# TensorE matmuls that nobody reads, issued ahead of its long waits, in a two-layer hybrid decoder trunk

## The reference

```python
for l in range(DEPTH):                       # DEPTH = 2
    h = rms_norm(x, norm_mix[l])
    p = h @ w_in[l]                          # RWKV-7 | gated DeltaNet | sparse MLA | 3 gates
    y_a = rwkv7_branch(...)
    y_b = gated_deltanet_branch(...)
    y_c = dsa_mla_branch(...)
    x = x + (g_a * y_a + g_b * y_b + g_c * y_c) @ w_mix_out[l]
    x = x + memory_xattn(rms_norm(x, norm_xattn[l]), mem_n, ...)
    h = rms_norm(x, norm_ffn[l])
    if l % 2 == 0:
        x = x + swiglu(h, w_gate, w_up, w_down)          # 2816 wide
    else:
        x = x + moe_swiglu(h, router, ...)               # top 2 of 8 experts, each 3584 wide
return rms_norm(x, final_norm)
```

## Time and profile before

| what | value |
|---|---|
| median of 3 runs | 2955.32 us (2954.4 to 2958.49) |
| profiled execution, first to last instruction (span) | 2958.0 us |
| mean granted TensorE clock over the span | 0.954 of 2.4 GHz |
| PE busy | 2588.5 us (88%) |
| VectorE (DVE) busy | 1706.3 us (58%) |
| ScalarE (ACT) busy | 1469.3 us (50%) |
| GpSimd (POOL) busy | 358.2 us (12%) |
| DMA | 531.34 MB, mean 180 GB/s |

### The profile page before, as it was taken

The page is one execution under the profiler, slowest core; times in us unless marked ns, Lnnn a source line. Parts: engine busy times, 40 slices in busy tenths (PEclk is TensorE's granted clock), DMA queues, the critical chain, the costliest instruction groups (busy, mean ns, idle before and its releaser), DMA issues.

```text
span 2958.0 us, 67158 instructions
## 1 busy us (share of the span) xinstructions
PE 2588.5 (88%) x29799; PEld 2117.4 (72%) x29818; DVE 1706.3 (58%) x1983; ACT 1469.3 (50%) x1911; POOL 358.2 (12%) x180
## 2 busy tenths in 40 slices
PE   7988988899797989897988999787898898998986
PEld 6766666777465768665666777557888888888875
DVE  2445463234215542545462233128999999999996
ACT  2233343233224331433343233137888889888885
POOL 0000001000000000000001000001323243324231
PEclk9999999999998999998989999898999999999999
DMA  6411120123216634301121133237999999999994
GB/s 201 135 41 47 31 86 29 37 93 114 95 62 228 202 119 139 100 30 31 58 63 32 58 107 100 100 125 289 388 386 386 386 386 388 382 386 390 385 387 183
DMA packets 304032, 531.34 MB, mean 180 GB/s; under 512 B 18528, under 2 KB 145760, under 8 KB 303360
## 3 DMA queue, kind: packets, MB, share of 16 engines
q1 hardware_dynamic: 303600, 525.99, 50.3%
q10 hardware_dynamic: 144, 1.05, 0.1%
HBM read 524.91 MB, written 2.10 MB: 178 GB/s over the span
## 4 chain that ended last, share of the span: by engine, by line
PE 53%; DVE 33%; ACT 7%; issue 6%; DMA 0%; ACTq 0%; DVEq 0%; SPq 0%
DVE arena L2713 24%; PE bank L799 11%; PE bank L700 9%; PE bank L770 4%; PE bank L1277 4%; PE bank L1236 4%; PE bank L765 3%; PE bank L718 2%; DVE yacc L2721 2%; PE bank L1293 2%; PE bank L644 2%; PE bank L1025 1%; ACT arena L1897 1%; PE bank L875 1%; PE bank L1030 1%
## 5 line engine op out<-in xcount | busy, mean ns | idle before, releaser
L2713 DVE TENSOR_TENSOR arena<-ring,arena 128x2048 bf16<-128x2048 f32 x336 | 833.4, 2525 | 3.8 <-ACT arena L2012 3.8
L2012 ACT ACTIVATE arena<-ring 128x2048 bf16<-128x2048 f32 x336 | 640.4, 1911 | 98.9 <-DMA ring<-in_moe_w_down 30.2
L1378 PE MATMUL bank<-arena 128*128 128x0 bf16 x10752 | 490.6, 209 | 99.4 <-DVE arena L2713 96.3
L1378 PEld LDWEIGHTS bank<-arena 128*128 128x128 bf16 x10752 | 478.6, 100 | 113.7 <-DVE arena L2713 105.3
L799 PE MATMUL bank<-feat,ring 128*128 128x256 f32 x1664 | 433.6, 399 | 8.4 <-ACT ring L1575 2.3
L1527 POOL TENSOR_TENSOR arena<-yacc,arena 128x512 bf16<-128x512 f32 x112 | 300.2, 2692 | 1004.5 <-ACT arena L2035 1004.5
L799 PEld LDWEIGHTS bank<-feat,ring 128*128 128x128 f32 x1664 | 308.6, 196 | 87.3 <-issue 43.1
L1395 PEld LDWEIGHTS bank<-arena 128*128 128x128 bf16 x5376 | 237.8, 98 | 23.0 <-issue 20.0
L1395 PE MATMUL bank<-arena 128*128 128x0 bf16 x5376 | 245.0, 206 | 7.3 <-issue 3.8
L700 PE MATMUL bank<-feat,ring 128*128 128x256 f32 x1056 | 236.8, 388 | 7.7 <-issue 5.7
L700 PEld LDWEIGHTS bank<-feat,ring 128*128 128x128 f32 x1056 | 205.7, 195 | 38.2 <-ACT feat L1566 8.9
(11 more groups left out here) (355 smaller groups left out, 3434.5 us busy)
## 6 DMA issues: line engine op xcount, KB each, us to landing
ring<-in_moe_w_gate SPq DMA_DIRECT2D x112, 1024.0 KB, 8.4
ring<-in_moe_w_up SPq DMA_DIRECT2D x112, 1024.0 KB, 7.9
ring<-in_moe_w_down SPq DMA_DIRECT2D x112, 1024.0 KB, 8.4
ring<-in_w_in SPq DMA_DIRECT2D x76, 1024.0 KB, 5.2
ring<-in_xa_w_kv SPq DMA_DIRECT2D x16, 1024.0 KB, 5.3
ring<-in_ffn_w_gate SPq DMA_DIRECT2D x11, 1024.0 KB, 5.4
ring<-in_ffn_w_up SPq DMA_DIRECT2D x11, 1024.0 KB, 5.4
ring<-in_ffn_w_down SPq DMA_DIRECT2D x11, 1024.0 KB, 7.0
```

The source lines that it names most:

```text
L1378: m = mm(o, w[k // 4][wi][:, k % 4, col:col + P], xg[:, e % 2, xi, k, :].shape_from_register(width[e % 2]), start=i == 0 and k == 0, stop= ...
L2012: sc.activation(w_parts[b][0], ring[:, b * FFN_SLOT:(b + 1) * FFN_SLOT], ACT.Copy).then_inc(S["w_hi"], 1)
L2713: v.tensor_tensor(w_parts[b][1], ring[:, b * FFN_SLOT:(b + 1) * FFN_SLOT], w_parts[b][0], ALU.subtract).then_inc(S["w_lo"], 1)
```

## The change

A helper `unread(n, b)` issues n float32 matmuls of the identity with the 128x512 mask into PSUM bank b. No engine waits for them and none reads what they write. Calls stand at these places of TensorE's program: 8 ahead of the first norm of layer 1; 4 ahead of each norm before the cross attention and before the feed-forward or routing, in both layers; 5 at the opening of DeltaNet, in both layers; 4 ahead of the wait for `ml_n`, in both layers; 8 ahead of the wait for `merged`, in both layers; 11 ahead of the dense feed-forward; 2 ahead of the wait for `mo_m` and 2 ahead of the gathers. That is 73 matmuls. No other instruction is added, removed or moved on any engine, and no DMA changes.

```diff
+            def unread(n, b):
+
+                for _ in range(n):
+                    mm(bk(b), C("ident"), C("cumask"), start=True, stop=True)
+
-            def norm(used=True):
+            def norm(used=True, spare=0):
+                unread(spare, 2)
                 for t, done in enumerate(("norm_x0", "norm_xn")):
                     pe.wait_ge(S[done], c.need(done))
...
             def gdn(l):
+                unread(5, 1)
                 pe.wait_ge(S["gd_g"], c.need("gd_g"))
                 pe.wait_ge(S["gd_ab"], c.need("gd_ab"))
...
+                unread(4, 4)
                 pe.wait_ge(S["ml_n"], c.need("ml_n"))
...
+                unread(2, 2)
                 pe.wait_ge(S["mo_m"], 1)
...
+                unread(2, 2)
                 pe.wait_ge(S["mo_xg"], 4)
...
             for l in range(LAYERS):
-                norm()
+                norm(True, 8 if l else 0)
                 pe_s.phase()
                 rwkv(l)
                 mla(l, gdn(l))
+                unread(8, 2)
                 pe.wait_ge(S["merged"], c.need("merged"))
                 to_residual(yacc)
-                norm()
+                norm(True, 4)
                 xattn(l)
-                norm()
+                norm(True, 4)
                 pe_s.phase()
                 if l == 0:
+                    unread(11, 3)
                     ffn(FF // 256)
```

## The result

The change takes 2932.62 us (median, 2930.4 to 2935.97) against 2954.86 us before: ratio 0.9922, 95% interval 0.9908 to 0.9936, 22 us faster. The direction was right and the size was not: 13 us had been forecast, and the time lies 0.6 us inside the lower end of the range.

The account below looks back on a forecast made before the run. For the first 2000 us TensorE's speed and its waits were taken to be on the path, with work behind waits at clock 0.50. Terms summed to 14.9 us, taken as 13 from the median: 2942.3 us, range 2932 to 2952.

Parts of the forecast that it names:

- What one new matmul costs: All places: 0.43 us each at 2.4 GHz, 0.86 at 1.2 GHz; 73 make 31 us of work meant for waits.
- When the clock falls: TensorE's waits: the clock falls surely over some 4 us, and in about half of cases between 2 and 3 us.
- Terms 1 and 2: Merge waits and layer 1's first norm: 5.0 and 4.7 us stay idle, the clock falls, gain 0.
- Terms 3 to 5: Norms ahead of cross attention, norms ahead of feed-forward and routing, `ml_n`: clock holds in half; 3.3, 1.2 and 3.0 us.
- Term 6: Eleven ahead of the dense feed-forward: some 2 us left, clock holds in half; gain 1.35 us, other end -0.6.
- Term 7: DeltaNet's opening: delay largely hidden by ScalarE, faster clock afterwards; 4.5 us for both layers, ends -3 and +6.
- the forecast's own signs of being wrong: Clock 0.50 behind all shortened waits, DeltaNet's line 1025 over a microsecond late, or expert stage taking back the front end's gain.
- Term 8: Routing, two and two: the 32 gathers, 6.42 us, take half at full clock; 3.2 us or nothing, taken as 1.5.
- The rule weighed: Norms' transposes: a skill's rule that transposes don't raise the clock; it would make the sum 10.4 us.
- Held everywhere: Rival, chance 0.13: the clock holds wherever 2 to 3 us are left; 27.6 us gained, 2928 us.
- Nothing comes of it: Rival, chance 0.20: clock falls in the waits' rest or unread writes don't count; 2955 us, from 2950 to 2957.
- Slower: Rival, chance 0.05: new matmuls run into the work, chiefly at DeltaNet's opening, 1.5 us lost per layer; 2960 us.

Follow-up runs that it names:

- The fours alone: The change with only the four matmuls ahead of each of four norms and both `ml_n` waits, zero elsewhere: 2947.09 us against 2954.86 before.
- the kernel with twice as many: The change with eight instead of four matmuls ahead of the four norms and both `ml_n` waits: 2948.06 us against 2956.74 before.
- the fastest kernel: The change plus matmuls ahead of ten RWKV-7 waits, DeltaNet's five moved ahead of the wait for `gn_y`: 2910.54 us against 2955.72 before.

## Why the prediction was right in direction and wrong in size

**What one new matmul costs: the step that failed.** The forecast took half of the true cost. "56 float32 matmuls of 128x512 take 24.20 us at 2.4 GHz, so 0.43 us each ... 73 of them are 31 us of work." The 0.43 us is right for a matmul of the trace. The 73 are matmuls of the program. The trace of the changed kernel has 146, so a program's matmul costs 0.86 us and the change 63 us. That could have been seen beforehand: in front of line 1025 the program has one matmul and the earlier trace rows say x2. So the waits were nearly full where the forecast had left 2.3 to 5.0 us of them open, and its terms 1 to 5 were worked out for waits that this kernel does not have. That the kernel with half the columns, whose matmuls do cost 0.43 us, comes to 2942.85 us where 2942.3 had been forecast is luck: `ml_n` gave 6.0 us for 3.0, the norms ahead of the cross attention lost 1.7 us for a gain of 3.3, and 9 of the 15.5 us by which its span is shorter lie outside the table's places. The Trainium skill, FP8 and Floating Point Precision, TensorE Precision Notes, says that a true float32 product takes four passes through the array. 84 bf16 matmuls of 256 columns take 9.33 us in the changed kernel, 0.11 us each, so four passes over 512 columns would be 0.89 us, an estimate by that rule, and the trace agrees: 7.03 us for eight.

**When the clock falls: right in the main.** Where some 4 us of a wait were left open the clock fell, where about 2 us were, it fell in some cases; the kernel with half the columns lost it at the merge and at both norms ahead of the cross attention, and held it at `ml_n`. Where the change left 0.5 to 1.3 us of a wait, the clock held each time.

**Terms 1 and 2 (merge, first norm of layer 1): 0 forecast.** These were mis-sized by the same cost. With 0.8 and 1.3 us left instead of 5.0 and 4.7 the clock held: 1.7, 1.7 and 3.2 us in the table, 7 to 8 us alone.

**Terms 3 to 5 (norms and `ml_n`): half of the price forecast, 7.5 us.** In the change they gave the whole: 2.2 + 3.9 for the norms ahead of the cross attention (6.6 had been the price), 3.0 + 3.0 at `ml_n`, and the transposes at 1.97 us in the others.

**Term 6 (feed-forward): 1.35 us forecast.** Together with the norm ahead of it 3.4 us in the change. The fours alone gave 2.0 of them. The overrun that was named as an end came true (9.68 us into 8.9). Alone, where they start at 1.2 GHz, the eleven gave 1.2 us in the trace and nothing that the runs can tell.

**Term 7 (DeltaNet): 4.5 us forecast, none seen.** In the trace layer 0 lost 1.9 us and layer 1 won 0.3. The place was read rightly: behind the wait for `gn_y`, with the clock gone in layer 0, though not in layer 1. With 6.20 and 4.56 us for the five instead of 2.2 to 4.3 the delay outran ScalarE's cover by 2.3 and 0.7 us, and the clock that was to stay at 1.00 fell again in the wait ahead of the second pair (1.86 us in layer 0). Moved ahead of the wait for `gn_y`, the five start in time. One of the forecast's own signs of being wrong came true here: line 1025 was not to start late by more than a microsecond, and in layer 0 it did.

**Term 8 (routing): 1.5 us forecast, 0.6 us seen in the traces.** The gathers did get faster by 2.5 us, but TensorE then waited 1.4 us longer for what comes next, and whatever is left is too small for the runs to tell.

**The rule weighed.** Transposes behind covered waits ran at 1.00, and the projections behind them too. That does not decide whether transposes count, since the new matmuls stood in front. No run separates the two.

**The rivals.** "Held everywhere" (2928 us, chance 0.13) comes nearest to what happened, but for another reason than its own: not that 2 to 3 us left open were harmless, but that only 0.5 to 1.3 us were left. DeltaNet and most of the routing fell short of it, and the merge, the first norm of layer 1 and untouched stretches made up for that, so that the time is near its 2928 us is in part luck. "Nothing comes of it" needed waits left open for the clock to fall in. "Slower" had a right mechanism in the wrong size: seen in layer 0's DeltaNet, and at full size in the kernel with twice as many.

## What to carry to other kernels

Count instructions in the trace, not in the source, before pricing one: here a float32 matmul is two. Issue unread matmuls so that they start with the wait and leave about a microsecond of it. Too few let the clock fall, what is too much is paid in full, and behind another wait they come too late. Look for short waits inside stages, too: ten places in a recurrence, in front of waits of 2.56 to 5.06 us, gave almost as much as all those between stages.

## What was new about the hardware

- Here a float32 matmul of 128x512 is executed as two of 0.43 us each at 2.4 GHz (146 records for 73 matmuls, 7.03 us for eight); one of 128x256 as two of 0.22 us. A float32 transpose is executed as one (16 records for the 16 of a norm).
- Waits of 0.5 to 1.3 us behind such a block kept the clock at 1.00 in all places of the change. Behind a wait of 2.04 us the clock stayed at the norms of the changed kernel and fell in the kernel with the fours alone; it fell behind 2.12 us at DeltaNet's opening in the fastest kernel.
- The unread matmuls did not slow VectorE, also with 36 more of them in RWKV-7, some 31 us of work: it was busy for 1704.7 us in the changed kernel and for 1703.1 us in the fastest, 1706.3 us before.
